# A two-block transformer kernel on one core: the even layer's low rank projection from unsplit fp32 operands, other ring places for later weights, the first gate group's products in another order

## The chip, the core and the metric

The kernel runs on one NeuronCore of a Trainium2 chip. The metric is the device time of one execution, in microseconds (us). Beside it stands one profiled execution, whose trace gives every instruction's start and duration on TensorE (PE, with its weight loads apart as PEld), VectorE (DVE), ScalarE (ACT), GpSimd (POOL) and the DMA queue of SyncE (SP).

## What is computed

The input has 256 tokens of width 1024. The reference runs two blocks. The first is a mixing layer (attention and spatial gating) followed by a feed-forward layer of 16 experts, of which each takes 32 tokens. The second has an even layer and an odd layer. The even layer is the one that the change touches:

```python
def mla_swa_layer(x, positions, g_in, w_in, g_q_a, w_q_up, g_kv_a, w_kv_up, sinks, w_out):
    h = rms_norm(x, g_in)
    z = h @ w_in
    cq, ckv, kpe, q_s, k_s, v_s, gate = split_cols(z, EVEN_SPLITS)   # 256, 128, 32, 512, 128, 128, 1024
    q = (rms_norm(cq, g_q_a) @ w_q_up) ...      # 8 heads of 96
    kv = (rms_norm(ckv, g_kv_a) @ w_kv_up) ...  # 8 heads of 64 + 64
    o_mla = causal_block_attention(qm, km, v_m)
    o_swa = sliding_window_sink_attention(q_s, k_s, v_s, sinks, alibi_slopes(SWA_HEADS))
    o = concatenate([o_mla, o_swa])
    return x + (o * silu(gate)) @ w_out
```

`cq`, `ckv` and `kpe` together are the 416 columns of the low rank projection, called `("e","a")` in the kernel; the queries of the sliding window are `("e","qs")`, its keys and values `("e","kvs")`, and the gate's two halves `("e","g1")` and `("e","g0")`. The two upward projections are `("qup",)` and `("kvup",)`, the output projection `("out2",0)` and `("out2",1)`. The odd layer has units named `("o",...)` and the same gate code.

## The kernel before, in words

**Weights and places.** All weights stream from HBM through a ring of seven places (`ring`, 16 KB of each partition a place), in one fixed order, `unit_of`, which SP issues (L765): each load waits until the unit that owned its place before is used. The experts' weights are plain fp32. The second block's weights are multiplied in another way: each is split into a high part (ACT rounds it, `hi_piece`, L454) and a low part (the rest, `lo_piece`, L466, on DVE or POOL), and a product is the sum of three matmuls, high by high, low by high and high by low (`products`). The high part goes to a second place `hslot`; the low part replaces the weights. A unit therefore takes two places until it is used, and before the change the pairs are `PAIRS`, in turn (3,2), (5,6), (0,1). The activations are split alike: `HE` is (high by ACT at L2016, low by DVE at L1582). The norm's scale is not in `HE`; it is applied to results later (`ra`, `RB`).

**The beginning of the even layer.** When the last expert's product is copied out (L514), PE scatters it to the tokens (L1022), DVE adds it to the transposed residual `XT` in eight pieces of 256 tokens (L1547), and then, piece by piece in the order `KORD`, ACT makes the high activation and a square (L2017), ACT and DVE split the weights of `("e","a")`, DVE makes the low activation. PE multiplies the first 128 tokens piece by piece as they come (L1072, group `("za",0)`), with the matmuls that sum the squares (L1080, two columns each, group `ss`) set between. The second 128 tokens follow (`project`, L496). Then PE runs, in program order: `qst` (`straight`, L508, two groups of 48 matmuls with the rows of the norm, L1090, between), three pairs of transposes, `kst` (L1105), `vst` (L1111), `qup` and `kvup` (L496), and one group of the gate (`gate_matmuls`, L690, four quarters of 12 matmuls). After that it transposes queries and keys (L485) and runs the attention `A2`, with the other gate quarters set between its steps.

**Order on the other engines.** ACT: high parts of `qs`, squares of `za` (L2025), the norm rows (L2029), high parts of `kvs`, `qup`, `kvup`, high part of `CT` (L2037), the copy of `vst` (L516), the copies of the query parts (L2045) with the four pieces of `g1` between, `kvup`'s copies, the pieces of `g0`. POOL: two short steps for the norm, then the low parts of `qup`, `kvup`, `g1`, `g0` and `out2` 0, in steps of 256 columns (16 for each of the last three). A quarter of the gate waits for the low parts of its four input pieces.

## Time and profile before

| | |
|---|---|
| runs | 1386.92 us median of 3 (1386.84 to 1388.49) |
| profiled execution | 1388.61 us, span of the trace 1386.8 us |
| PE, PEld busy | 72%, 37% of the span |
| DVE, ACT, POOL busy | 29%, 17%, 6% |
| HBM read | 480.43 MB, 347 GB/s over the span |
| chain that ended last | DMA 55%, PE 33%, DVE 6%, ACT 3% |

From about 160 us to 1089 us the experts' weights arrive at some 428 GB/s and the transfers set the pace. From 1089 us on the kernel is paced by its engines: the even layer lasts to about 1227 us, the odd layer to the end. Every time below is in us from the start of the span. A PE busy for all of a stretch is not a PE at its peak; the granted clock beside it, 1.00 or 0.50, is the 2.4 or the 1.2 GHz level.

### The profile page before, as it was taken

What the parts mean: (1) busy time and instruction counts of PE and PEld (TensorE: products, weight loads), DVE (VectorE), ACT (ScalarE), POOL (GpSimd) and SP (SyncE); (2) the same over time, 40 slices, a digit from 0 to 9 for tenths busy, and PEclk for the clock granted to TensorE, in tenths of its full rate; (3) what the DMA queues carried; (4) which work ended last, traced back from release to release, by engine and by line L of the source; (5) the groups of instructions that cost most, each with busy time, mean ns of one, the idle gap of its engine ahead of it and who ended that gap; (6) DMA issues with size and microseconds to landing.
All of it is one profiled execution on the core that took longest, in us unless ns stands there. A gap on an engine that the chain in (4) does not pass through costs nothing.

```text
span 1386.8 us, 15261 instructions
## 1 busy us (share of the span) xinstructions
PE 992.9 (72%) x6623; PEld 510.2 (37%) x6623; DVE 396.3 (29%) x954; ACT 239.4 (17%) x483; POOL 89.6 (6%) x129
## 2 busy tenths in 40 slices
PE   4998987666666665566566565666656798899987
PEld 3765842212121111111111111111111487899875
DVE  4756421011111100101011010101101455775584
ACT  3534210000000000000000000000000355643452
POOL 1300000000020000000000000000000044300030
PEclk9999989878887887977888877788877798999998
DMA  9996789999999999999999999999999552144411
GB/s 398 375 378 237 317 362 428 428 429 426 429 427 427 430 427 427 429 427 428 429 428 427 428 428 426 430 428 427 428 427 428 216 184 98 62 182 146 159 62 46
DMA packets 34771, 482.47 MB, mean 348 GB/s; under 512 B 3854, under 2 KB 3856, under 8 KB 5520
## 3 DMA queue, kind: packets, MB, share of 16 engines
q1 hardware_dynamic: 34240, 479.92, 82.7%
q8 instruction: 52, 0.85, 0.2%
q10 hardware_dynamic: 288, 1.05, 0.2%
q0 software_dynamic: 176, 0.53, 0.1%
q14 instruction: 15, 0.12, 0.0%
HBM read 480.43 MB, written 1.05 MB: 347 GB/s over the span
## 4 chain that ended last, share of the span: by engine, by line
DMA 55%; PE 33%; DVE 6%; ACT 3%; issue 1%; POOL 1%; SPq 0%; POOLq 0%; DVEq 0%; ACTq 0%
DMA ring<-in_t_w 52%; PE PS L508 8%; PE PS L1009 6%; PE PS L496 6%; PE PS L1055 3%; DMA ring<-in_t_e_a 2%; DMA ring<-in_t_mod 2%; ACT S L624 1%; PE PS L690 1%; PE PS L485 1%; PE PS L997 1%; PE PS L786 1%; POOL RR L466 1%; PE PS L1022 1%; PE PS L808 1%
## 5 line engine op out<-in xcount | busy, mean ns | idle before, releaser
L1009 PE MATMUL PS<-ring,S 128*32 128x512 f32 x2016 | 320.7, 770 | 213.4 <-DMA ring<-in_t_w 210.9
L1055 PE MATMUL PS<-ring,S 128*32 128x512 f32 x1008 | 168.7, 803 | 103.7 <-DMA ring<-in_t_w 94.8
L1009 PEld LDWEIGHTS PS<-ring,S 128*32 128x32 f32 x2016 | 63.0, 126 | 447.7 <-DMA ring<-in_t_w 329.4
L514 DVE COPY S<-PS 128x512 f32<-128x512 f32 (+2 forms) x47 | 32.1, 682 | 307.9 <-PE PS L1055 287.7
L508 PE MATMUL PS<-SR,RR 128*128 128x256 f32 x736 | 117.5, 285 | 1.2 <-DVE ab L1441 0.9
L1055 PEld LDWEIGHTS PS<-ring,S 128*32 128x32 f32 x1008 | 33.3, 130 | 223.0 <-DMA ring<-in_t_w 147.6
L508 PEld LDWEIGHTS PS<-SR,RR 128*128 128x128 f32 x736 | 103.8, 189 | 2.6 <-DVE ab L1441 1.2
L454 ACT ACTIVATE RR<-ring 128x1024 fp32r<-128x1024 f32 (+3 forms) x95 | 89.5, 1005 | 37.8 <-DMA ring<-in_t_e_a 18.1
L1557 DVE TENSOR_SCALAR S<-PS,KC 128x256 f32<-128x256 f32 x16 | 7.7, 483 | 287.0 <-PE PS L1039 287.0
L516 ACT ACTIVATE S<-PS 128x512 f32<-128x512 f32 (+2 forms) x50 | 27.9, 568 | 340.8 <-PE PS L485 335.9
L466 DVE TENSOR_TENSOR RR<-ring,RR 128x1024 fp32r<-128x1024 f32 (+2 forms) x76 | 84.1, 1154 | 8.5 <-ACT RR L454 8.5
L2004 ACT ACTIVATE S<-PS 128x512 f32<-128x512 f32 x16 | 9.6, 597 | 440.8 <-PE PS L1009 440.8
L496 PE MATMUL PS<-RR,SR 128*128 128x512 f32 (+3 forms) x264 | 76.9, 402 | 0.0
L1567 DVE TENSOR_TENSOR S<-PS,S 128x512 f32<-128x512 f32 x16 | 11.1, 691 | 204.2 <-PE PS L1009 204.2
L485 PE MATMUL PS<-KC,S 128*128 128x128 f32 (+1 forms) x308 | 44.5, 289 | 27.8 <-DVE S L1272 14.8
L508 PE MATMUL PS<-RR,RR 128*128 128x256 f32 x224 | 62.9, 281 | 0.0
L466 POOL TENSOR_TENSOR RR<-ring,RR 128x256 fp32r<-128x256 f32 x74 | 52.5, 743 | 126.3 <-ACT RR L454 126.3
L1547 DVE SCALAR_TENSOR_TENSOR X<-PS,ab,X 128x256 f32<-128x256 f32 x128 | 51.9, 476 | 21.8 <-PE PS L1022 21.8
L690 PE MATMUL PS<-SR,RR 128*128 128x256 f32 x256 | 52.4, 304 | 5.2 <-POOL RR L466 4.6
L485 PEld LDWEIGHTS PS<-KC,S 128*128 128x128 f32 (+1 forms) x308 | 35.7, 146 | 54.9 <-DVE S L1567 35.3
L496 PEld LDWEIGHTS PS<-RR,SR 128*128 128x128 f32 x264 | 51.3, 197 | 11.2 <-issue 0.3
L2173 POOL TENSOR_TENSOR st<-st,KC 128x4 f32<-128x4 f32 x1 | 1.9, 1947 | 714.0 <-DVE st L1591 714.0
(309 smaller groups left out, 986.5 us busy)
## 6 DMA issues: line engine op xcount, KB each, us to landing
ring<-in_t_w SPq DMA_DIRECT2D x189, 2048.0 KB, 31.3
ring<-in_t_mod SPq DMA_DIRECT2D x12, 2048.0 KB, 12.7
ring<-in_t_out SPq DMA_DIRECT2D x6, 2048.0 KB, 7.8
S<-in_t_w SPq DMA_DIRECT2D x3, 2048.0 KB, 12.2
ring<-in_t_e_g SPq DMA_DIRECT2D x2, 2048.0 KB, 7.8
ring<-in_t_o_q SPq DMA_DIRECT2D x2, 2048.0 KB, 7.8
ring<-in_t_o_k SPq DMA_DIRECT2D x2, 2048.0 KB, 8.8
ring<-in_t_o_v SPq DMA_DIRECT2D x2, 2048.0 KB, 8.2
```

The costliest lines, as they stand in the source:

```text
L454: act.e.activation(hi[:, c:c + step, :], dst[:, c:c + step, :], ACT.Copy).then_inc(*act.mark(("hi", key, c)))
L466: t = lane.e.tensor_tensor(lo[:, k, w], place[key][:, k, w], hi[:, k, w].bitcast(F32), ALU.subtract)
L485: t = pe.e.transpose(PS[0:parts, b, 128 * i:128 * i + 128], in_, ident)
L496: m = pe.e.matmul(PS[:, b, 0:width], l_, r_, start=(k == ks[0] and n == 0), stop=(k == ks[-1] and n == 2))
L508: m = pe.e.matmul(PS[:, b, 256 * nn:256 * nn + 256], l_, r_, start=(k == ks[0] and m_ == 0), stop=(k == ks[-1] and m_ == 2))
L514: lane.e.tensor_copy(dst, src).then_inc(*lane.mark(out_of(key), *names))
L516: lane.e.activation(dst, src, ACT.Copy).then_inc(*lane.mark(out_of(key), *names))
L624: t = act.e.activation(p[:, c], p[:, c], ACT.Exp, bias=nm[:, i_:i_ + 1], scale=-1.0, accum_out=sm[:, i_:i_ + 1])
L690: m = pe.e.matmul(PS[:, b, 256 * nn:256 * nn + 256], l_, r_, start=(k == 0 and m_ == 0), stop=(k == 7 and m_ == 2))
L1009: m = pe.e.matmul(PS[32 * j:32 * j + 32, b, :], expert_rows(2 * k + kk, e_, e_ + 1), place[name, e_, k][:, kk, 512 * j:512 * j + 512], sta ...
L1055: m = pe.e.matmul(PS[q:q + 32, b, :], HT[e_ % 2][:, 128 * s + 32 * j:128 * s + 32 * j + 32], place["w2", e_, j][:, s, 512 * dh:512 * dh + ...
L1547: t = dve.e.scalar_tensor_tensor(out=XT[:, k, :], in0=PS[:, banks.of[key], o:o + 256], scalar=ab[:, 7, k:k + 1], in1=XT[:, k, :], op0=ALU. ...
```

## The change

Three edits.

1. **Low rank projection.** The unit `("e","a")` is not split. ACT multiplies its eight pieces (128 by 416, fp32) in place by the gain `gfe`, which used to be in the activations, as soon as the unit has landed. PE multiplies plain fp32 `XT` by these weights: one matmul a piece and token half in the place of three. The order on PE becomes `za` 0, all the square sums, `za` 1. ACT makes the weights, then the four squares, then the eight high activations; DVE adds all eight pieces first and makes the low activations afterwards. The first user of `HE` is then `qst`, which waits for it.
2. **Places.** The later units go to other places: `("e","a")` to 3 alone, `qs` (5,6), `kvs` 0 with both parts, `qup` and `kvup` (1,2), and then (3,5), (6,0), (1,2) in turn. `qup`'s load now follows the last expert unit's use, `g1`'s the use of `("e","a")`, `g0`'s that of `qs`.
3. **Gate.** In the first group of the gate, the quarters are 0 and 1: high by high and high by low activation, for all eight pieces, one output half each; 2 and 3: the low weights by the high activation. The first two wait for the high parts alone. The high pieces of `g1` are now made all together on ACT before the copy of `vst`. The odd layer's first gate group has the same new order.

```diff
-    for n, (key, w) in enumerate(later):
+
+    LATER = [(3, None), (5, 6), (0, 0), (1, 2)] + [((3, 5), (6, 0), (1, 2))[n % 3] for n in range(len(later) - 4)]
+    for (key, w), (slot, hslot) in zip(later, LATER):
         k_ = 2 if key == ("qup",) else 8
-        unit(key, unit_rows("t_" + "_".join(map(str, key)), k_, w), k_, w, *PAIRS[n % 3])
+        unit(key, unit_rows("t_" + "_".join(map(str, key)), k_, w), k_, w, slot, hslot, hoff=2048 if slot == hslot else 0)
...
+                lead = half == halves[0] and n2 == 0
                 for q in range(4):
...
-                    nn = q // 2
+                    nn = q % 2 if lead else q // 2
                     n = 2 * n2 + nn
-                    for k in range(4 * (q % 2), 4 * (q % 2) + 4):
-                        pe.wait_ge(("split", ukey, k))
...
+                    for k in range(8) if lead else range(4 * (q % 2), 4 * (q % 2) + 4):
+                        pe.wait_ge(("hi", ukey, k - k % 2) if lead and q < 2 else ("split", ukey, k))
+                        hi_hi, lo_hi, hi_lo = products(ukey, h, k, slice(128 * n, 128 * n + 128), slice(0, 256), swap=True)
+
+                        group = [hi_hi, lo_hi, hi_lo] if not lead else [hi_hi, hi_lo] if q < 2 else [lo_hi]
...
+        def low_rank(i):
+
+            b = banks.take(("za", i), ALL6)
+            pe.wait_ge(banks.was["za", i])
+            for k in KORD:
+                pe.wait_ge(("weighted", k), ("xa", E - 1, k))
+                m = pe.e.matmul(PS[:, b, 0:416], XT[:, k, 128 * i:128 * i + 128], place["e", "a"][:, k, :], start=k == KORD[0],
+                                stop=k == KORD[-1])
+            m.then_inc(*pe.mark(("za", i), *([used(("e", "a"))] if i else [])))
+
+        low_rank(0)
+        for i in range(2):
+            banks.take(("ss", i), ALL6)
...
         m.then_inc(*pe.mark("ss"))
-        project(pe, ("za", 1), ("e", "a"), HE, 1, 416, ks=KORD, final=True)
+        low_rank(1)
...
-            straight(pe, ("qst", n2), ("e", "qs"), HE, n2, final=n2 == 1)
+            straight(pe, ("qst", n2), ("e", "qs"), HE, n2, final=n2 == 1, first="he")
...
-            lo_piece(dve, ("e", "a"), (0, 4, 2, 6)[c])
-            for k in (c, 4 + c):
-                dve.wait_ge(("he hi", k), "gg", ("xa", E - 1, k))
...
+        for k in KORD:
+            dve.wait_ge(("he hi", k), "gg", ("xa", E - 1, k))
...
         act.stage("even")
-        hi_piece(act, ("e", "a"), 0)
-        hi_piece(act, ("e", "a"), 4)
+        act.wait_ge(("load", ("e", "a")), "gg")
+        for k in KORD:
+            w = place["e", "a"][:, k, :]
+            act.e.activation(w, w, ACT.Copy, scale=gfe[:, k:k + 1]).then_inc(*act.mark(("weighted", k)))
         for c in range(4):
-            for k in (c, 4 + c):
-                act.wait_ge(("xa", E - 1, k), "gg")
-                act.e.activation(HE[0][:, k, :], XT[:, k, :], ACT.Copy, scale=gfe[:, k:k + 1]).then_inc(*act.mark(("he hi", k)))
+            act.wait_ge(("xa", E - 1, c), ("xa", E - 1, 4 + c))
...
+        for k in KORD:
+            act.e.activation(HE[0][:, k, :], XT[:, k, :], ACT.Copy, scale=gfe[:, k:k + 1]).then_inc(*act.mark(("he hi", k)))
         hi_all(act, ("e", "qs"))
...
+        hi_all(act, ("e", "g1"))
         act.wait_ge("vst", ("rcs", 0), ("rcs", 1))
         copy_out(act, "vst", VST, PS[:, banks.of["vst"], 0:256], "vst rows")
...
-            hi_piece(act, ("e", "g1"), 4 * i)
-            hi_piece(act, ("e", "g1"), 4 * i + 2)
```

## Rows read from the trace of the kernel before

**Rows 1.** The page's strips, 40 equal slices: PE clock in tenths, DMA.
```profile
PEclk9999989878887887977888877788877798999998
DMA  9996789999999999999999999999999552144411
```

**Rows 2.** The chain of waits in time order: start, duration, engine and line.
```profile
1059.71 29.61 DMA ring<-in_t_e_a
...
1114.55 5.74 PE PS L508 x48
...
1135.74 0.95 ACT RR L454
1136.76 11.56 POOL RR L466 x16
1148.36 6.37 PE PS L690 x30
...
1303.20 5.77 PE PS L690 x48
```

**Rows 3.** Busy time of PE, PEld, DVE, ACT, POOL; granted clock; DMA; by stretch.
```profile
1092.50:1099.50 7.00, 4.71 (x27) 4.21 (x27) 7.00 (x15) 5.57 (x11) 0.00 (x0) 1.00 0.19 76
1099.50:1106.90 7.40, 7.35 (x29) 7.22 (x30) 2.01 (x3) 3.92 (x5) 0.00 (x0) 0.50 0.00 0
1106.90:1113.10 6.20, 6.20 (x19) 5.92 (x20) 4.72 (x11) 1.02 (x4) 3.24 (x3) 0.50 0.00 0
...
1114.20:1140.30 26.10, 26.10 (x198) 25.21 (x197) 16.01 (x51) 13.04 (x26) 11.84 (x17) 1.00 0.57 212
1140.30:1143.80 3.50, 1.82 (x13) 1.43 (x11) 1.92 (x3) 3.50 (x12) 3.50 (x6) 1.00 0.72 215
...
1148.40:1154.10 5.70, 5.70 (x27) 5.70 (x28) 0.00 (x0) 0.00 (x0) 5.70 (x9) 0.50 0.00 0
```

**Rows 4.** Timeline, PE and its weight loads in the low rank projection.
```profile
1089.41 2.00 PE L1022 MATMUL PS<-S 64*128 64x256 f32 x16 [0.79 <-DVE S L514]
...
1095.58 0.60 PEld L1080 LDWEIGHTS PS<-st,S 128*128 128x128 f32 x4
...
1100.41 1.11 PEld L1080 LDWEIGHTS PS<-st,S 128*128 128x128 f32 x4
...
1113.26 0.54 PE L496 MATMUL PS<-RR,SR 128*128 128x416 f32 x2
...
1113.82 0.54 PE L496 MATMUL PS<-RR,SR 128*128 128x416 f32 x2
```

**Rows 5.** Timeline, PE: four plain fp32 matmuls of 256 columns and what follows.
```profile
1176.98 2.00 PE L1148 MATMUL PS<-S 96*128 96x256 f32 x8
1178.62 0.59 PE L690 MATMUL PS<-SR,RR 128*128 128x256 f32 x2
```

**Rows 6.** Timeline, ACT and DVE as the even layer begins.
```profile
1089.34 1.68 ACT L454 ACTIVATE RR<-ring 128x832 fp32r<-128x832 f32 x2 [18.06 <-DMA ring<-in_t_e_a]
...
1090.16 0.88 DVE L1547 SCALAR_TENSOR_TENSOR X<-PS,ab,X 128x256 f32<-128x256 f32 x2 [0.81 <-PE PS L1022]
...
1090.93 0.89 ACT L2016 ACTIVATE SR<-X,st 128x256 fp32r<-128x256 f32 x2
```

**Rows 7.** Timeline, ACT and POOL before the gate.
```profile
1127.15 1.21 ACT L2037 ACTIVATE SR<-PS,KC 128x256 fp32r<-128x256 f32 x3 [0.78 <-PE PS L485]
1133.31 0.39 ACT L516 ACTIVATE S<-PS 128x256 f32<-128x256 f32 x1 [4.95 <-PE PS L1111]
...
1124.76 7.02 POOL L466 TENSOR_TENSOR RR<-ring,RR 128x256 fp32r<-128x256 f32 x10 [7.62 <-ACT RR L454]
```

**Rows 8.** The page's DMA issues, the gate's two units: KB, us to landing.
```profile
ring<-in_t_e_g SPq DMA_DIRECT2D x2, 2048.0 KB, 7.8
```

**Rows 9.** Timeline, DVE: one step with POOL at rest, then with POOL busy.
```profile
1176.81 0.62 DVE L639 TENSOR_SCALAR S<-S,st 128x256 f32<-128x256 f32 x2
...
1182.10 1.58 DVE L639 TENSOR_SCALAR S<-S,st 128x256 f32<-128x256 f32 x2
```

More of the change, by code:

```diff
@@ L280, in body @@
     FIRST = (3, 4, 2, 7, 8, 5, 6, 0, 1, 9)
-    PAIRS = ((3, 2), (5, 6), (0, 1))
     n_u, borrowed = 0, {}
@@ L295, in body @@
     later += [(("o", n), 512) for n in ("q0", "q1", "k0", "k1", "v0", "v1", "g0", "g1")] + [(("out3", h), 512) for h in range(2)]
-    for n, (key, w) in enumerate(later):
+    LATER = [(3, None), (5, 6), (0, 0), (1, 2)] + [((3, 5), (6, 0), (1, 2))[n % 3] for n in range(len(later) - 4)]
+    for (key, w), (slot, hslot) in zip(later, LATER):
         k_ = 2 if key == ("qup",) else 8
-        unit(key, unit_rows("t_" + "_".join(map(str, key)), k_, w), k_, w, *PAIRS[n % 3])
+        unit(key, unit_rows("t_" + "_".join(map(str, key)), k_, w), k_, w, slot, hslot, hoff=2048 if slot == hslot else 0)
         if key == ("qup",):
-            unit(("kvup",), unit_rows("t_kvup", 1, 1024), 1, 1024, *PAIRS[n % 3], off=1536, hoff=1536, share=key)
+            unit(("kvup",), unit_rows("t_kvup", 1, 1024), 1, 1024, slot, hslot, off=1536, hoff=1536, share=key)
     def used(key):
@@ L683, in gate_matmuls @@
                         pe.wait_ge(banks.was[key])
-                    nn = q // 2
+                    nn = q % 2 if lead else q // 2
                     n = 2 * n2 + nn
-                    for k in range(4 * (q % 2), 4 * (q % 2) + 4):
-                        pe.wait_ge(("split", ukey, k))
-                        for m_, (l_, r_) in enumerate(products(ukey, h, k, slice(128 * n, 128 * n + 128), slice(0, 256),
-                                                               swap=True)):
-                            m = pe.e.matmul(PS[:, b, 256 * nn:256 * nn + 256], l_, r_, start=(k == 0 and m_ == 0),
-                                            stop=(k == 7 and m_ == 2))
+                    for k in range(8) if lead else range(4 * (q % 2), 4 * (q % 2) + 4):
+                        pe.wait_ge(("hi", ukey, k - k % 2) if lead and q < 2 else ("split", ukey, k))
+                        hi_hi, lo_hi, hi_lo = products(ukey, h, k, slice(128 * n, 128 * n + 128), slice(0, 256), swap=True)
+                        group = [hi_hi, lo_hi, hi_lo] if not lead else [hi_hi, hi_lo] if q < 2 else [lo_hi]
+                        for m_, (l_, r_) in enumerate(group):
+                            m = pe.e.matmul(PS[:, b, 256 * nn:256 * nn + 256], l_, r_,
+                                            start=k == 0 and m_ == 0 and (q == 0 or not lead),
+                                            stop=k == 7 and m_ == len(group) - 1 and (q == 3 or not lead))
                     if q == 3:
@@ L1063, in pe_program @@
         pe.stage("even")
-        for name in (("za", 0), ("ss", 0), ("ss", 1)):
-            banks.take(name, ALL6)
-        pe.wait_ge(banks.was["za", 0])
-        for n in range(len(KORD) + 2):
-            if n < len(KORD):
-                k = KORD[n]
-                pe.wait_ge(("split", ("e", "a"), k), ("he", k))
-                for m_, (l_, r_) in enumerate(products(("e", "a"), HE, k, slice(0, 416), slice(0, 128))):
-                    m = pe.e.matmul(PS[:, banks.of["za", 0], 0:416], l_, r_, start=(n == 0 and m_ == 0),
-                                    stop=(n == len(KORD) - 1 and m_ == 2))
-                if n == len(KORD) - 1:
-                    m.then_inc(*pe.mark(("za", 0)))
-            if n >= 2:
-                c, dh = KORD[n - 2] % 4, KORD[n - 2] // 4
-                pe.wait_ge(("sqs", c), "gg", *[banks.was["ss", i] for i in range(2)])
-                for i in range(2):
-                    m = pe.e.matmul(PS[:, banks.of["ss", i], 0:2], sqs[:, c, 256 * dh + 128 * i:256 * dh + 128 * i + 128],
-                                    gg[:, KORD[n - 2], :], start=n == 2, stop=n == len(KORD) + 1)
+        def low_rank(i):
[9 more added lines that the diff above has]
+            banks.take(("ss", i), ALL6)
+        for i in range(2):
+            pe.wait_ge(banks.was["ss", i])
+        for k in KORD:
+            c, dh = k % 4, k // 4
+            pe.wait_ge(("sqs", c), "gg")
+            for i in range(2):
+                m = pe.e.matmul(PS[:, banks.of["ss", i], 0:2], sqs[:, c, 256 * dh + 128 * i:256 * dh + 128 * i + 128],
+                                gg[:, k, :], start=k == KORD[0], stop=k == KORD[-1])
         m.then_inc(*pe.mark("ss"))
-        project(pe, ("za", 1), ("e", "a"), HE, 1, 416, ks=KORD, final=True)
+        low_rank(1)
         def spread_rows(name, n):
```

9 lines of the change are left out of this document (4 added, 5 removed).

## The prediction

> **What bounds the kernel now.** I read the strips first. The transfers are full until the 31st of 40 slices and thin after it, and the clock digit dips until there too [rows 1]: up to about 1089 us the weights set the pace, and nothing of the change touches that, since the units up to the last expert keep their places and their order. The chain of waits then says where the engines take over: the transfer of `("e","a")` ends at 1059.71 + 29.61 = 1089.32, and from there the chain is PE work with two breaks. One is the low rank projection, which ends where `qst` begins, at 1114.4 us on the timeline (the chain, which counts to the end of the last matmul, has 1114.55). The other is POOL: sixteen low pieces of `g1`, 11.56 us, and PE after them at 1148.36 [rows 2]. Third, the table by stretch. In 1092.5 to 1099.5 PE is busy 4.71 of 7.00 us while DVE is busy 7.00 of 7.00: DVE makes two kinds of low part and adds besides. From 1099.5 to 1113.1 PE is full but at clock 0.50. From 1114.2 to 1140.3 it is full at clock 1.00, 26.10 of 26.10. Then the gate: half idle (1.82 of 3.50), and at clock 0.50 up to 1154.1 [rows 3]. So between 1089.4 and 1154.7 there are two places to gain in, and 26 us between them that only move.
>
> **Part 1, the low rank projection.** It removes the eight splits of `("e","a")` on ACT and DVE, 48 matmuls of the split form and every wait of PE for a low part here. It adds eight ACT steps of 128 by 416 and 16 plain fp32 matmuls of 416 columns.
>
> ACT: 128 by 832 takes 1.68 / 2 = 0.84 us, 128 by 256 takes 0.89 / 2 = 0.45 us [rows 6]; 416 lies between, about 0.55. They start with the landing at 1089.3, so the first is there at 1089.9 and the last at 1093.7. DVE's eight additions at 0.44 [rows 6] run from 1090.2 to 1093.7. PE is in the scatter from 1089.4 and free at about 1091.3 [rows 4]. So PE never waits for either: it takes a piece in more time than they do.
>
> PE: a plain fp32 matmul shows as two records. Eight records of 256 columns take 1178.62 - 1176.98 = 1.64 us, 0.205 each [rows 5]; for 416 columns that is 0.33. The split form shows 1113.82 - 1113.26 = 0.56 us for three matmuls of 416 columns at full clock [rows 4], 0.19 each. If the 128 by 128 fp32 weight load is not hidden behind the matmul before, 0.60 / 4 = 0.15 us comes on top [rows 4]: 0.48 a record. I take 0.36, near the lower end, since at [rows 5] the weight loads are of the same kind and are hidden. Then one token half is 16 x 0.36 = 5.8 us against 24 x 0.19 = 4.5: PE has 2.6 us more work, and the reason for a gain is the waits alone. The squares' matmuls are paced by their weight loads, 32 x 0.15 = 4.8 us at full clock and 32 x 0.28 = 9 us at half [rows 4]; their operands are there (four squares on ACT after 1093.7, about 0.6 each, to 1096.1).
>
> At full clock: 1091.3 + 5.8 + 4.8 + 5.8 = 1107.7 for the first matmul of `qst`, 6.7 us sooner than 1114.4. `qst` needs the high and low activations and split weights: ACT 1096.1 + 8 x 0.45 = 1099.7, DVE just behind, then the `qs` pieces on ACT to 1103.6 and on DVE to about 1106.5, each piece before PE wants it. The norm's chain starts from the end of the squares, 1101.9 where it was 1107.1, so the rows are ready too.
>
> **The clock** takes part of this back. It fell at 1099.5 after a stretch in which PE worked 4.71 of 7.00 us, two-column matmuls among them. It then stayed at 0.50 through 7.40 us in which PE was 7.35 us busy, mostly alternating with the squares' matmuls, and came back only after 6.2 us of dense 416-column work; the gate's stretch shows the same, 5.7 us dense before the rise [rows 3]. That PE was busy was thus not enough there, and the squares' matmuls were much of what it did. The change puts 4.8 us of them in one block. I expect the clock to fall in that block or at its end, and to come back after some 6 us of `za` 1. Those 6 us do 3 us of work: 3.0 lost. If the fall comes in the middle of the block, its second half costs 1.8 more. I take the mean, 3.9 lost: `qst` at 1111.6, **2.8 us sooner**. The bounds are 6.7 sooner (no fall) and 10.8 later (below).
>
> Here the Trainium skill speaks otherwise ("TensorE: Matmul & The Clock Gate", section "Why this matters for your kernels"): keep TensorE continuously busy, without long idle gaps, and the clock stays up. The new order has no idle gap, so by it there is no fall. The trace agrees in part: it shows a full clock in the 26 us without gaps, but also half clock through a stretch with PE busy. I follow the trace, and give the rule's result as a rival.
>
> **Part 2, places.** No work is added, only loads come sooner. `g1` waits for the use of `("e","a")` (1111.6 or before) and lands 7.8 us later [rows 8], at 1119.4, where it is wanted at about 1125. Its high parts need the place of `qs`, used at the end of `qst`, before that as well. `g0` follows `qs` and lands by about 1132; wanted at 1138. From `out2` on each unit waits for the same unit as before, so the rest of the rotation costs and brings nothing. Early loads share the queue with nothing that is awaited: price 0; if `g1` were late, ACT would stand at its high parts with the copy of `vst` and all query copies queued behind it, and 4 us of slack would have to go first.
>
> **Part 3, the gate.** Times in this part are those of before; all of it moves by 2.8. ACT stands idle from the high part of `CT`, done at 1128.4, to `vst` at 1133.3 [rows 7]. The four high pieces of `g1` at 0.97 fit, 1128.4 to 1132.3. POOL ends its first ten steps at 1124.76 + 7.02 = 1131.8 [rows 7] and goes on with `g1` at once, 5 us sooner than 1136.76: 11.56 us [rows 2], done at 1143.3. PE reaches the gate at 1140.3 [rows 3] and has 32 matmuls that want high parts only, 32 x 0.12 = 3.8 us, to 1144.1. By then all low parts are there, and the other 16 end at 1146.1. As a whole that is 5.77 us, as the same 48 matmuls without a wait take in the odd layer [rows 2]. Before, the group ended at 1148.36 + 6.37 = 1154.73 [rows 2], or 1154.6 by starts, so it took 14.3 us. **8.5 us sooner**, of which about 2.8 us is that the clock no longer falls here. What is late next: the query copies on DVE end at 1140.7 and the key parts at 1142.2, both ahead of 1146.1; ACT, rid of the interleaved pieces, ends its copies at 1141. The attention follows as it stood, and its low parts of `g0` are ready sooner relative to it. In the odd layer the group already runs without a wait [rows 2], so the new order gives 0 there.
>
> **POOL beside DVE.** POOL now works from 1131.8 to 1136.8, where it rested and DVE scales the residual in eight steps of two SBUF operands. The trace shows what such company can cost: a pair of DVE steps takes 0.62 us with POOL at rest and 1.58 with it busy [rows 9], 0.5 each. Eight steps would lose about 4 us, of which the slack to 1146.1 hides nearly all. I take 0.5 us, with 0 and 2 as ends. The Trainium skill ("SBUF — State Buffer", section "SBUF: two separate sides") says that a DVE step with two SBUF inputs and a GpSimd step that reads SBUF lock each other out entirely. By that POOL too would lose eight DVE steps of 0.4 us, 3.2 us, and quarter 3 would wait; the sum would be some 1.5 us smaller. No row shows POOL much slowed: 0.70 a step beside DVE, 0.72 here.
>
> **Sum.** 2.8 + 8.5 - 0.5 = 10.8 us. The profiled execution, 1388.6 us, would become 1377.8. The median of the runs was 1386.92, 1.7 us under it, and a new median should be **1376.1**.
>
> **Rivals.**
> - *The clock holds.* No fall in the block of squares: 3.9 us more gain, 1372.2. For it: PE is dense for 5.8 us before the block. Against: the fall at 1099.5 and the low stretch with PE full [rows 3].
> - *The gate gains less.* POOL starts `g1` no sooner, because the high parts come late or DVE holds it up: then the low parts end at 1148.4, PE follows with the last matmuls to 1149.5, and the gain is 5.1 in the place of 8.5: 1379.5. So would it be if the change failed to do what it says.
> - *Plain fp32 is dearer.* Weight loads in the open, 0.48 a record: 32 x 0.12 = 3.9 us more, 1380.0.
> - *Slower.* The clock is low from the scatter to the end of the projection. Then 1.9 + 11.6 us of work double to 27 and the squares take 9: 1089.4 + 36 = 1125.2, 10.8 later than 1114.4, less 8.0 from the gate: 2.8 us slower, 1389.7. It decides from about 14.5 us of loss to the clock, and needs nearly the whole stretch at 0.50. Before, only 13.6 us of it were.
>
> **How the numbers follow.** Forecast 0.53, clock holds 0.22, gate gains less 0.11, dearer fp32 0.10, slower 0.04. The range takes in the first two with the ends of the clock's loss and the third and fourth: 1371.8 to 1380.2, which leaves out something under 2 in 10. About 0.2% of the time, 2.8 us, is what a measurement can tell from no change. All cases but the last are faster by more than that; with something for cases that I do not see: faster 0.93, same 0.03, slower 0.04.
>
> **What would show it.** `qst`'s first matmul near 1111.6 (1107.7 if the clock holds), and two-column matmuls in one block with the clock falling in or right behind it. PE without a wait from 1091.3 on. POOL's low parts in one run of 26 steps with no idle before `g1`. The gate's first group about 5.8 us long at full clock, and the transposes behind it near 1143.8. Wrong would be: fp32 records of 416 columns over 0.4 us apart, ACT waiting before `vst`, PE waiting in quarter 2, or a new loss in the attention that eats what was won.

## The result, and the profile after

The changed kernel took 1378.55 us, the median of six runs (1376.87 to 1384.31), beside 1386.88 us for the kernel before, run beside it (six runs, 1386.84 to 1388.56): a ratio of 0.9942, interval 0.9925 to 0.9959. Run again beside the experiments it had 1379.43 and 0.9934 [0.9917, 0.9951]. So it is about 8.3 us faster by the medians and 8.0 by the ratio (5.7 to 10.4), where 10.8 were forecast. The time lies in the range, 2.4 us above the number. That small distance is in part luck: it hides errors that cancel in part.

The page of the kernel after: the span, the busy engines, the strips and the shares of the chain.

```profile
span 1382.5 us, 15237 instructions
...
PE 993.8 (72%) x6607; PEld 505.7 (37%) x6607; DVE 397.5 (29%) x950; ACT 240.9 (17%) x487; POOL 91.1 (7%) x129
...
PEclk9999989788787788778687887888887899999999
DMA  9896789999999999999999999999999733154411
...
DMA 55%; PE 35%; DVE 6%; ACT 3%; issue 1%; SPq 0%; POOL 0%; POOLq 0%; DVEq 0%; ACTq 0%
```

The page alone says little: as in [rows 1] the transfers are full up to the 31st slice. This profiled execution, 1384.31 us, was the slowest of the six; those of the experiments lie up to 8 us apart from it. The comparison is therefore made by stage. Each stage below is read off the timeline by first starts, so that the sum of a line is the span: the end of DVE's copy of the last expert's product; from there to the first matmul of `qst`; from `qst` to the first matmul of the gate; the gate's first group; the rest. The last column is the span less the first, which is free of how soon the weights came in that execution (1088.0 to 1091.8 us, by the execution and not by the edit).

| profile | copy ends | to `qst` | to gate | gate group | rest | from copy to end |
|---|---|---|---|---|---|---|
| before | 1089.4 | 25.0 | 25.9 | 14.3 | 232.2 | 297.4 |
| after | 1091.8 | 19.9 | 31.5 | 5.6 | 233.6 | 290.7 |
| e5_changed_again | 1089.4 | 19.9 | 31.6 | 5.7 | 233.3 | 290.5 |
| e2_pool_later | 1088.2 | 19.8 | 26.3 | 12.8 | 235.0 | 293.9 |
| e4_places_gate_only | 1089.5 | 27.4 | 29.7 | 5.7 | 233.5 | 296.5 |
| e3_low_rank_only | 1088.0 | 19.9 | 26.2 | 13.5 | 231.8 | 291.4 |
| e1_scaling_later | 1088.8 | 16.5 | 26.2 | 5.7 | 238.5 | 286.9 |
| e7_scaling_split | 1088.8 | 20.0 | 26.2 | 6.1 | 235.9 | 288.2 |
| e11_scaling_split_again | 1090.0 | 19.8 | 26.2 | 6.1 | 234.2 | 286.3 |
| e8_old_gate_order | 1089.2 | 16.5 | 31.4 | 5.7 | 233.5 | 287.2 |
| e9_split_old_order | 1088.5 | 16.5 | 26.3 | 9.6 | 233.8 | 286.2 |
| e6_squares_last | 1088.4 | 16.8 | 34.5 | 5.7 | 233.5 | 290.5 |
| e10_squares_between | 1091.5 | 16.5 | 27.9 | 5.9 | 232.8 | 283.0 |

Two stages gained, 5.1 and 8.7 us, and the one between them, where nothing was to happen, lost 5.6: 8.2 in all. The rest took 1.4 us more, so that from the copy on the profile is 6.7 us shorter; in e5_changed_again it is 6.9. The medians differ by 8.3. The chain of waits of the kernel after shows them (start, duration, engine and line; L1075 is the low rank projection, L1088 the squares' matmuls, L509 `qst`, L497 `kvup`, L694 the gate):

```profile
1091.10 0.70 DVE S L515
1091.85 2.00 PE PS L1027 x16
1093.85 5.78 PE PS L1075 x16
1099.63 4.41 PE PS L1088 x32
1104.04 8.10 PE PS L1075 x16
1112.14 5.71 PE PS L509 x48
...
1129.76 6.75 DVE X L1642 x8
1136.51 0.63 DVE st L525
1137.24 0.63 DVE st L527
...
1139.48 3.90 PE PS L497 x9
1143.38 5.63 PE PS L694 x48
1149.01 3.53 PE PS L486 x32
...
1299.44 5.71 PE PS L694 x48
```

From the copy on PE goes from the scatter into the projection, the squares and the projection again without a gap, where [rows 3] had PE busy 4.71 of 7.00 us. The gate's 48 matmuls follow one another in 5.63 us; the POOL step of [rows 2] that they used to wait for is gone from the chain. The odd layer's group takes 5.71, against 5.77 in [rows 2]. New in the chain are 6.75 us of DVE at L1642, which scales the residual.

The windows of the kernel after, columns as in [rows 3], give the clock:

```profile
1093.80:1099.50 5.70, 5.70 (x20) 3.15 (x18) 2.85 (x9) 5.70 (x13) 0.00 (x0) 1.00 0.69 285
1099.50:1103.90 4.40, 4.40 (x33) 4.40 (x32) 3.69 (x8) 4.40 (x8) 0.00 (x0) 0.78 0.08 33
1103.90:1108.80 4.90, 4.90 (x8) 2.50 (x9) 4.57 (x11) 1.96 (x5) 3.24 (x3) 0.50 0.00 0
1108.80:1111.70 2.90, 2.90 (x11) 1.59 (x9) 0.15 (x1) 0.39 (x2) 0.00 (x0) 1.00 0.00 0
...
1135.80:1139.50 3.70, 0.17 (x2) 0.02 (x1) 3.67 (x13) 0.76 (x3) 3.70 (x6) 1.00 0.01 2
1143.20:1148.80 5.60, 5.60 (x49) 5.58 (x48) 0.00 (x0) 4.44 (x6) 3.71 (x6) 1.00 0.81 284
```

The clock is full in `za` 0, falls in the block of squares (a mean of 0.78), stays at 0.50 into `za` 1 and is back by 1108.8. The fifth line is the new wait: PE works 0.17 of 3.70 us while DVE and POOL are both full.

### The profile page after: what moved, and what is told of

It reads as the page before. It is cut to its first block, busy times and chain, and to the rows that moved or that the text cites. A ratio compares the mean times of both kernels' runs of the same rounds, so it can differ in the third digit from the quotient of the medians.

```text
span 1382.5 us, 15237 instructions
## 1 busy us (share of the span) xinstructions
PE 993.8 (72%) x6607; PEld 505.7 (37%) x6607; DVE 397.5 (29%) x950; ACT 240.9 (17%) x487; POOL 91.1 (7%) x129
## 4 chain that ended last, share of the span: by engine, by line
DMA 55%; PE 35%; DVE 6%; ACT 3%; issue 1%; SPq 0%; POOL 0%; POOLq 0%; DVEq 0%; ACTq 0%
DMA ring<-in_t_w 54%; PE PS L509 8%; PE PS L1014 6%; PE PS L497 5%; PE PS L1060 3%; DMA ring<-in_t_mod 2%; PE PS L486 1%; PE PS L694 1%; ACT S L625 1%; PE PS L1075 1%; PE PS L1027 1%; PE PS L791 1%; PE PS L1002 1%; PE PS L813 1%; PE PS L589 1%
## 5 line engine op out<-in xcount | busy, mean ns | idle before, releaser
L509 PE MATMUL PS<-SR,RR 128*128 128x256 f32 x736 | 118.0, 286 | 1.0 <-DVE ab L1449 0.9
L509 PEld LDWEIGHTS PS<-SR,RR 128*128 128x128 f32 x736 | 104.3, 190 | 2.5 <-DVE ab L1449 1.2
L455 ACT ACTIVATE RR<-ring 128x1024 fp32r<-128x1024 f32 (+2 forms) x91 | 85.9, 1006 | 20.0 <-DMA ring<-in_t_o_v 17.0
L467 DVE TENSOR_TENSOR RR<-ring,RR 128x1024 fp32r<-128x1024 f32 (+1 forms) x72 | 80.1, 1162 | 8.6 <-ACT RR L455 8.6
L497 PE MATMUL PS<-RR,SR 128*128 128x512 f32 (+2 forms) x248 | 70.7, 397 | 3.5 <-DVE S L1659 3.5
L509 PE MATMUL PS<-RR,RR 128*128 128x256 f32 x224 | 63.2, 282 | 0.0
L497 PEld LDWEIGHTS PS<-RR,SR 128*128 128x128 f32 x248 | 46.7, 191 | 14.8 <-DVE S L1659 4.0
L694 PE MATMUL PS<-SR,RR 128*128 128x256 f32 x256 | 49.8, 293 | 0.6 <-DVE SG L743 0.6
```

Of the source, the lines that this page charges most:

```text
L455: act.e.activation(hi[:, c:c + step, :], dst[:, c:c + step, :], ACT.Copy).then_inc(*act.mark(("hi", key, c)))
L467: t = lane.e.tensor_tensor(lo[:, k, w], place[key][:, k, w], hi[:, k, w].bitcast(F32), ALU.subtract)
L497: m = pe.e.matmul(PS[:, b, 0:width], l_, r_, start=(k == ks[0] and n == 0), stop=(k == ks[-1] and n == 2))
L509: m = pe.e.matmul(PS[:, b, 256 * nn:256 * nn + 256], l_, r_, start=(k == ks[0] and m_ == 0), stop=(k == ks[-1] and m_ == 2))
L694: m = pe.e.matmul(PS[:, b, 256 * nn:256 * nn + 256], l_, r_, start=k == 0 and m_ == 0 and (q == 0 or not lead), stop=k == 7 and m_ == len( ...
```

## The experiments

### Where the middle stretch lost

PE's timeline names the releaser (start, duration, line, operation, output and operands, count, and in brackets the wait before it), DVE's and POOL's show what they did. First the kernel after:

```profile
1139.48 1.22 PE L497 MATMUL PS<-RR,SR 128*128 128x512 f32 x2 [3.53 <-DVE S L1659]
...
1129.76 6.75 DVE L1642 SCALAR_TENSOR_TENSOR X<-X,KC,cvec 128x256 f32<-128x256 f32 x8
1136.43 0.71 DVE L525 TENSOR_TENSOR st<-S,rcs 128x32 f32<-128x32 f32 x1
...
1122.33 19.91 POOL L467 TENSOR_TENSOR RR<-ring,RR 128x256 fp32r<-128x256 f32 x26 [7.59 <-ACT RR L455]
```

then the same two kinds of DVE step in the kernel before, where POOL was at rest:

```profile
1132.19 3.26 DVE L1635 SCALAR_TENSOR_TENSOR X<-X,KC,cvec 128x256 f32<-128x256 f32 x8
1135.37 0.18 DVE L524 TENSOR_TENSOR st<-S,rcs 128x32 f32<-128x32 f32 x1
```

Beside POOL the eight scaling steps take 6.75 us in place of 3.26, and a rotary step of 32 columns 0.71 in place of 0.18 (three of the six such steps do; the three between them keep 0.18). Steps of the same stretch that read one operand from PSUM are not slowed: those of 80 columns take 0.23 to 0.24 us beside POOL and without it. Behind them DVE copies and rotates the queries, which frees the PSUM banks of `qup`; `kvup` takes one of these banks, and PE waits 3.53 us for it. The theory: POOL, which now makes the low parts of `g1` 5 us sooner, holds up DVE, and that holds up PE by a bank. The rival: the wait comes from the new places or the late start of the projection.

**e1_scaling_later** moves the eight scaling steps out of the way.

```diff
-        dve.wait_ge(*[("sqs", c) for c in range(4)], *[("he", k) for k in range(8)])
-        for k in range(8):
-            t = dve.e.scalar_tensor_tensor(out=XT[:, k, :], in0=XT[:, k, :], scalar=c_gf[:, k:k + 1], ...)
-        t.then_inc(*dve.mark("x2"))
...
         dve.wait_ge(out_of(("kvup", 1, 1)))
         t.then_inc(*dve.mark("km"))
+        dve.wait_ge(*[("sqs", c) for c in range(4)], *[("he", k) for k in range(8)])
+        for k in range(8):
+            t = dve.e.scalar_tensor_tensor(out=XT[:, k, :], in0=XT[:, k, :], scalar=c_gf[:, k:k + 1], ...)
+        t.then_inc(*dve.mark("x2"))
```

> The changed kernel with DVE's eight scaling steps of the residual (x2) moved behind the key parts. Theory A (in the changed kernel the scaling, slowed by POOL beside it, keeps DVE from freeing the banks of the query projection, and PE waits 3.5 us for a bank in the key and value projection): the wait is gone, from the first matmul of qst to the first of the gate it is 26 us again in the place of 31.6, and the time falls by about 5 us against the changed kernel, to some 1373 us. Rival B (PE's wait there is for something else, or the scaling only costs later what it cost before): still over 30 us from qst to gate or the loss found again before the attention, time within 1 us of the changed kernel's 1378.

**e2_pool_later** leaves DVE as it is and holds POOL instead, until DVE has made the key parts.

```diff
+        pool.wait_ge("km")
         lo_all(pool, ("e", "g1"))
```

> The changed kernel with POOL's low parts of g1 held back until DVE has made the key parts (km). Theory A (POOL is what slows DVE's scaling): the eight scaling steps take 3.3 us again in the place of 6.75, PE has no wait before the gate, but the gate's quarters 2 and 3 now wait for POOL, which ends some 11.5 us after the key parts; gate's end about 2 to 3 us later than in the changed kernel, time about 1380. Rival B (the scaling is slow for another reason, such as its place against ACT or PE): it stays at 6.75 us, and the time goes up by 6 us or more, to 1384 and over.

Measured: e1 1377.55 us, ratio 0.9932 [0.9909, 0.9955]; e2 1381.98, 0.9963 [0.9950, 0.9975]. DVE in e2, then in e1:

```profile
1126.18 3.26 DVE L1642 SCALAR_TENSOR_TENSOR X<-X,KC,cvec 128x256 f32<-128x256 f32 x8
1129.36 0.18 DVE L525 TENSOR_TENSOR st<-S,rcs 128x32 f32<-128x32 f32 x1
```

```profile
1132.59 7.12 DVE L1665 SCALAR_TENSOR_TENSOR X<-X,KC,cvec 128x256 f32<-128x256 f32 x8
1139.63 0.68 DVE L730 TENSOR_TENSOR SG<-PS,cvec 128x512 f32<-128x512 f32 x1
```

With POOL silent the steps are at their old 3.26 and 0.18 us, PE does not wait for a bank, and the stretch takes 26.3 us, with the places and the projection of the change. So POOL's company is the cause, and 5.2 us of the 5.6 hang on it. e1 takes the steps out of `kvup`'s path and has 26.2 too. But neither gives the whole gain. In e2 POOL is now late for the gate, which takes 12.8 us in place of 5.6, 6.8 us of it and of what follows at half clock:

```profile
1133.68 12.45 POOL L467 TENSOR_TENSOR RR<-ring,RR 128x256 fp32r<-128x256 f32 x18 [7.94 <-DVE S L1665]
...
1144.80 2.50 PE L694 MATMUL PS<-SR,RR 128*128 128x256 f32 x10 [2.23 <-POOL RR L467]
```

In e1 the steps are still beside POOL, 7.12 us, and now stand before DVE's first step on the gate (L730): from the end of the gate's group to the first exponential of the attention it takes 10.0 us in place of 7.4 (6.6 in e5). The 5 us over the change that were expected of e1 did not come: the median is 1.0 to 1.9 us under the changed kernel's two.

The 7.4 us are themselves 1.0 longer than in the kernel before (6.4), and that is POOL's company once more. A DVE step of four columns ahead of the first exponential, first after, then before:

```profile
1155.05 1.17 DVE L607 SCALAR_TENSOR_TENSOR st<-KC,st 128x4 f32<-128x4 f32 x1
```

```profile
1160.78 0.16 DVE L606 SCALAR_TENSOR_TENSOR st<-KC,st 128x4 f32<-128x4 f32 x1
```

In the kernel after POOL is still at the low parts of `g0`, until 1156.20, and the step ends at 1156.22; in the kernel before POOL had ended at 1159.32.

### The parts alone

**e4_places_gate_only** is the kernel before with edits 2 and 3 and the old projection; **e3_low_rank_only** is the kernel after with the old places and the old gate, `g1`'s high pieces between the query copies again. e4 against the kernel before, then e3 against the kernel after:

```diff
+    LATER = [(3, 2), (5, 6), (0, 0), (1, 2)] + [((3, 5), (6, 0), (1, 2))[n % 3] for n in range(len(later) - 4)]
+                    nn = q % 2 if lead else q // 2
...
+        hi_all(act, ("e", "g1"))
         act.wait_ge("vst", ("rcs", 0), ("rcs", 1))
```

```diff
-    LATER = [(3, None), (5, 6), (0, 0), (1, 2)] + [((3, 5), (6, 0), (1, 2))[n % 3] for n in range(len(later) - 4)]
+    LATER = [(3, None)] + [((3, 2), (5, 6), (0, 1))[n % 3] for n in range(1, len(later))]
...
-        hi_all(act, ("e", "g1"))
...
+            hi_piece(act, ("e", "g1"), 4 * i)
+            hi_piece(act, ("e", "g1"), 4 * i + 2)
```

> The kernel before with edits 2 and 3 alone (places, high parts of g1 together and earlier, new order in the first gate group; the low rank projection split as before, its high parts in place 2). Theory A (the gate's 8.5 us are won, but DVE beside POOL gives back 5 to 6 us before the gate): 3 us faster than before, 1384 us, with the scaling steps at over 6 us and a wait of PE of about 3.5 us before the gate. The prediction's own term (8.5 less 0.5): 8 us faster, 1379 us, with no wait before the gate.

> The kernel before with edit 1 alone (plain fp32 projection; the places of the other units, the high parts of g1 and the order in the gate as before). By the changed kernel's trace, in which qst began 19.9 us after the landing of the unit against 25.1 before: 5 us faster than before, 1382 us, and the gate's group at 14 us as before. By the prediction's own term: 2.8 us faster, 1384 us. A rival that the clock gives all of it back: 1386.9.

Measured: e4 1388.19 us, ratio 0.9995 [0.9981, 1.0009]; e3 1382.35, 0.9965 [0.9952, 0.9977]. The places and the gate alone bring nothing that can be measured, where 3 us were expected. In e4's profile the gate's group is 8.6 us shorter, the stretch before it 3.8 longer, and the projection 2.4 longer, with the clock low for 20.5 us from 1095.0 where it was low for 13.7 before. The longer projection, with that longer low stretch, is what the expectation did not have. The same wait as in the kernel after is there, with the old projection, so the new projection is not its cause; the new places are not either, since e2 has them and no wait:

```profile
1134.78 6.75 DVE L1640 SCALAR_TENSOR_TENSOR X<-X,KC,cvec 128x256 f32<-128x256 f32 x8
...
1144.51 0.73 PE L497 MATMUL PS<-RR,SR 128*128 128x512 f32 x2 [3.54 <-DVE S L1657]
```

The projection alone, e3, is worth 4.9 us by the ratio and 5.1 in its stage. Its chain, the scatter first and then the same 16, 32 and 16 records as above:

```profile
1088.01 3.70 PE PS L1024 x16
1091.71 5.78 PE PS L1072 x16
1097.49 3.47 PE PS L1085 x32
1100.96 7.39 PE PS L1072 x16
1108.35 5.71 PE PS L509 x48
```

The scatter takes 3.70 us in place of 2.00, because the clock was at 0.50 until 1091.5; behind the block it was low for 3.4 us more, against 6.8 in the kernel after.

From the copy to the end the profiles of the parts, 6.0 us shorter (e3) and 1.0 (e4), add up to about the change's 6.7. By the ratios, 4.9 and 0.7 against 8, they fall some 2.5 us short; e4's twelve runs lie between 1380.64 and 1391.54, so that this is not told from their spread.

### The same kernel again

**e5_changed_again** is the changed kernel without an edit, to see what of a profile repeats.

> The changed kernel once more, beside the next three on one chip. 8 us faster than the kernel before. From the first matmul of qst to the first of the gate 31 to 32 us, the gate's first group 5.7 us. Theory on its spread (1376.9 to 1384.3 us in six runs): the time from the landing of the last expert weights to qst differs from run to run with the place of the low clock, 17 us without one and 20 us with one; a rival is that the spread comes from the experts' stage alone.

Measured: 1379.43 us. Its stages repeat those of the first profile within 0.3 us, 19.9, 31.6 and 5.7; the copy ended 2.4 us sooner. So these stages are the kernel's own as far as two profiles can tell, and the landing of the weights is the execution's. The expectation set the spread of the runs down to a fall of the clock that comes in some executions only; both profiles have the fall, so that they do not decide it, and the copy alone moved by 2.4 us.

### Both engines apart: half of the scaling on each side

**e7_scaling_split**, and once more **e11_scaling_split_again**, put four scaling steps where POOL still rests, ahead of DVE's low parts of `kvs`, and four behind the key parts.

```diff
+        dve.wait_ge(("rb", "e"), *[("sqs", c) for c in range(4)], *[("he", k) for k in range(8)])
+        for k in range(4):
+            dve.e.scalar_tensor_tensor(out=XT[:, k, :], ...)
         lo_all(dve, ("e", "kvs"))
...
         t.then_inc(*dve.mark("km"))
+        for k in range(4, 8):
+            t = dve.e.scalar_tensor_tensor(out=XT[:, k, :], ...)
+        t.then_inc(*dve.mark("x2"))
```

> The changed kernel with the eight scaling steps split: four right before the low parts of kvs, where POOL rests, four behind the key parts. In the first experiment all eight behind the key parts took 7.1 us beside POOL and held the gate's first DVE step up by about 2 us. Theory A: the first four take 1.6 us, the last four 3.4 us or less and end before the gate's group does; PE has no wait before the gate (26 us from qst to gate), and transposes follow the group at once. 6 to 8 us faster than the changed kernel, about 1371 us. Rival: the low parts of kvs come later now, and PE waits for them in kst, up to 1 us, or the first four still meet POOL: then no better than the first experiment, within 1 us of its time.

> e7 once more, beside the two above. Theory (what e7 wins before the gate is kept, and its profile lost 3 us to two low stretches of the clock in the odd layer's attention by where they fell): 26.2 us from qst to gate, 6.1 for the group and 226 to 229 us from the first exponent to the end, median about 1376 to 1378, 10 to 12 us faster than before. Rival (the loss in the odd layer belongs to the schedule): 229 us again there.

Measured: 1378.81 us, 0.9922 [0.9908, 0.9937], and 1377.20, 0.9922 [0.9899, 0.9944]. DVE in e11:

```profile
1117.68 1.67 DVE L1620 SCALAR_TENSOR_TENSOR X<-X,KC,cvec 128x256 f32<-128x256 f32 x4 [2.76 <-ACT cvec L2039]
...
1137.51 3.60 DVE L1668 SCALAR_TENSOR_TENSOR X<-X,KC,cvec 128x256 f32<-128x256 f32 x4
```

One kernel holds both prices: 0.42 us a step with POOL at rest, 0.90 beside it. The stretch before the gate takes 26.2 us in both profiles, and the path from the gate to the first exponential 6.5, so nothing of e1's loss is left. From the copy to the end the profiles are 2.5 and 4.4 us shorter than that of the kernel after. Up to the first exponential both are 5.7 to 5.8 us ahead of the kernel after. The rest of it goes in low stretches of the clock in the odd layer, 10.2 us of them in e7 where the kernel after has 3.4; in e11, which has 3.4 there too, 1.0 us goes between the first exponential and the odd layer's gate and 0.5 behind it. By the ratios the gain over the change is 1.7 to 2.8 us, where 6 to 8 were expected of e7, and it is within the intervals.

### What the order of the gate's products is worth

**e8_old_gate_order** is the kernel after with the old order of the first group; **e9_split_old_order** is e7 with the old order.

```diff
-                    nn = q % 2 if lead else q // 2
+                    nn = q // 2
...
-                    for k in range(8) if lead else range(4 * (q % 2), 4 * (q % 2) + 4):
-                        pe.wait_ge(("hi", ukey, k - k % 2) if lead and q < 2 else ("split", ukey, k))
+                    for k in range(4 * (q % 2), 4 * (q % 2) + 4):
+                        pe.wait_ge(("split", ukey, k))
```

> The changed kernel with the old order of products in the gate's first group (each quarter waits for its low parts). Theory (as PE is held up before the gate anyway, POOL has ended g1's low parts at 1142.2 before the gate starts at 1143.2, so the order brings nothing): the group takes 5.7 us as in the changed kernel, time within 1 us of it. The prediction's own view, in which the group reaches high parts 3 us before the low parts are there: 1 to 3 us slower than the changed kernel.

> The kernel with the scaling split (four steps before the low parts of kvs, four behind the key parts) and the old order of products in the gate's first group. In e7, with the new order, PE came to the gate without a wait and the group took 6.1 us. Theory (now the order counts, since the high parts are there and POOL is not yet through with g1's low parts): the group takes 8 to 9 us here, 2 to 3 us more than in e7, and the transposes follow that much later. Rival (POOL is through before PE comes to the gate in this schedule too): 5.7 to 6.1 us, as in e7.

Measured: e8 1380.69 us, 0.9942 [0.9926, 0.9957], the ratio of the changed kernel itself; e9 1376.99, 0.9921 [0.9907, 0.9936], that of e7. In e8 the group takes 5.7 us with the old order. It begins at 1137.1, and POOL has the last low part of `g1` at 1136.3 (two of the 26 records are missing from the trace):

```profile
1117.84 18.46 POOL L467 TENSOR_TENSOR RR<-ring,RR 128x256 fp32r<-128x256 f32 x24
```

So in the change the sooner high and low parts did all of the gate's gain, and the new order had nothing to hide, because PE came late by the very wait that POOL caused. With PE on time the order does work in the profile: the group takes 9.6 us in e9, behind a wait for a low part, and 6.1 in e7 and e11.

```profile
1135.96 0.79 PE L692 MATMUL PS<-SR,RR 128*128 128x256 f32 x2 [2.34 <-POOL RR L467]
```

Part of these 3.5 us is a fall of the clock behind that wait (records of the same kind start 0.21 us apart at first and 0.12 later). The medians do not separate the two, so that the order is worth anything in the whole time stays unshown.

### The squares and the clock

Nine profiles have the block of squares between `za` 0 and `za` 1. In six of them (after, e2, e3, e5, e7, e11) the clock fell in the block or up to 1.1 us behind it, and `qst` came 19.8 to 20.0 us after the copy; in three (e1, e8, e9), with the same instructions on PE there, it held, and `qst` came after 16.5. Four of the six (after, e2, e5, e11) lose all of it to one low stretch of 6.8 us. In e3 and e7 the low stretch behind the block is 3.4 us, and the other half of the loss lies in the scatter, which ran at half clock. The block and `za` 1 in e1, columns as in [rows 3]:

```profile
1096.60:1100.10 3.50, 3.50 (x34) 3.50 (x33) 3.04 (x6) 3.50 (x7) 0.00 (x0) 1.00 0.07 28
1100.10:1105.30 5.20, 5.20 (x17) 2.81 (x17) 4.81 (x12) 2.78 (x6) 3.25 (x3) 1.00 0.00 0
```

 One theory: the block of two-column matmuls brings the fall. The rival: the fall has nothing to do with them. **e6_squares_last** moves the block behind `za` 1; **e10_squares_between** is e7 with the four matmul records of each piece's squares ahead of its `za` 1 piece. The two edits in turn:

```diff
         low_rank(0)
+        low_rank(1)
         for i in range(2):
             banks.take(("ss", i), ALL6)
...
         m.then_inc(*pe.mark("ss"))
-        low_rank(1)
```

```diff
+        for k in KORD:
+            pe.wait_ge(("sqs", k % 4), "gg")
+            for i in range(2):
+                m = pe.e.matmul(PS[:, banks.of["ss", i], 0:2], sqs[...], gg[:, k, :], ...)
+            m = low_rank_piece(1, k)
```

> The changed kernel with the block of the squares' matmuls behind the second half of the low rank projection. Theory C (the block of two-column matmuls makes the clock fall): where the clock falls, it falls in or behind the block, now in the first 6 us of qst, and costs the same 2 to 3 us there; time within 2 us of the changed kernel. Rival D (the fall has to do with the idle time before the scatter, and the block with nothing): the fall stays at the same distance from the scatter, now inside the projection's dense part. Both expect the norm's chain, 5.6 us later, to hold up nobody: it has the first group of qst as cover.

> e7 with the squares' matmuls set between the eight pieces of the second token half of the projection, four records before each piece, in the place of a block ahead of them. Theory C (it is the unbroken block of two-column matmuls that lets the clock fall; it fell in or behind it in six of eight profiles with the block ahead of a dense part): no fall before qst or a shorter one, from the copy of the last expert product to qst 16.5 to 17.5 us, where it was 19.9 to 20.0 with a fall. Rival D (their amount counts, wherever they stand, as in the kernel before, where they were set between and the clock fell too): a fall as before, 19.5 us or more to qst, perhaps longer than in the block's case.

Measured: e6 1381.33 us, 0.9943 [0.9931, 0.9956]; e10 1375.55, 0.9916 [0.9898, 0.9934]. The windows of e6 and then of e10, columns as before:

```profile
1090.50:1101.80 11.30, 11.30 (x34) 6.21 (x35) 6.44 (x14) 11.19 (x20) 0.00 (x0) 1.00 0.36 149
1101.80:1105.20 3.40, 3.40 (x34) 3.40 (x32) 0.00 (x0) 0.00 (x0) 0.00 (x0) 0.99 0.72 217
1105.20:1112.00 6.80, 6.58 (x30) 6.29 (x31) 4.72 (x11) 2.04 (x8) 3.51 (x5) 0.50 0.47 200
```

```profile
1091.50:1098.00 6.50, 6.49 (x29) 4.04 (x30) 3.30 (x9) 6.50 (x14) 0.00 (x0) 1.00 0.80 313
1098.00:1107.90 9.90, 9.90 (x51) 7.00 (x50) 4.64 (x11) 6.47 (x11) 0.00 (x0) 1.00 0.08 31
```

In e6 the projection runs at full clock through 11.3 us; then the block comes, PE busy 3.40 of 3.40 us, and the clock is at 0.50 right behind it, now in `qst`. The fall moved with the block: to `qst` 16.8 us in place of 19.9, to the gate 34.5 in place of 31.5. That the block brings the fall is thus shown once by moving it. In e10 there is no fall. But e1, e8 and e9 had none with the block whole, and before, with the same matmuls in between, it fell [rows 3]; so one profile does not show that the mixing prevents it. It has a price, too: the first group of `qst` now waits for DVE's low parts of `qs` and takes 7.3 us in place of 6.1, so that 1.6 us go before the gate (27.9 against 26.2).

Nor is it shown what decides between a fall and none for the same instructions. One thing divides the nine profiles, and no run varied it: in the six with a fall the block began 5.8 to 8.0 us after the clock had last come back to full, in the three without one 8.1 to 8.6 us. It is not a plain matter of more or less, since in e6 the block began 13.6 us after and the clock fell.

e10 has the best median of all, 1375.55 us, 3 to 4 us under the changed kernel's two (by the ratios, each to the kernel before on its own chip, 2.5 to 3.6), and its profile is the shortest from the copy to the end, 283.0 us. Its interval overlaps those of the others.

## Why the prediction was right or wrong

**What bounds.** Right in the main. The edits moved time between 1089 and 1155 us, as read from [rows 1 to 3]. But the rest of the kernel took 1.4 and 1.1 us more in the two profiles of the change, and 0.4 less in e3, and the prediction had it follow as it stood. Of the 1.4, 1.0 is the DVE step beside POOL ahead of the first exponential (0.2 of the 1.1 in e5_changed_again). From there to the odd layer's gate it takes 1.0 more in both profiles, and from that gate to the end 0.6 and 0.1 less. I did not settle what these are; the low stretches of the clock lie elsewhere in every profile there.

**Part 1, the projection: right mechanism, mis-sized.** PE without a wait, ACT's and DVE's steps off its path, and 5.8 us for a token half are there (5.78). The record of 0.36 us, taken from [rows 5] rather than with an open weight load, was right: they start 0.35 apart. Three terms were too dear. The squares take 3.47 us at full clock (e3), 0.11 a record, not 0.15: the 0.60 us of [rows 4] run to the end of the last of four loads, and three of these start 0.11 apart. That is 1.3 us. `za` 1 takes 5.35 us by starts (e1), not 5.8: 0.5. And the clock took 3.4 us (19.9 against 16.5 without a fall), not 3.9: 0.5 again. With these 2.3 the 2.8 us sooner become 5.1, and without a fall the 6.7 become 8.5. The clock fell where the prediction said, in or at the end of the block. By the Trainium skill ("TensorE: Matmul & The Clock Gate", section "Why this matters for your kernels") a TensorE kept busy would have kept its clock; the windows of after and e6 show a fall out of a stretch in which it was busy all of the time, e1, e8, e9 and e10 show none. The rival "the clock holds" is what three of the nine executions with the block did, and its price of 3.9 was 3.4.

**Part 2, places.** Priced at 0. No run changed the places alone; the only wait of PE before the gate in the profile after is the one for the bank. But the 0 hides what the places did. `g1` landed at 1134.70 in the kernel before, so that with the old places POOL could not have gone on to it at 1131.8; after, it landed at 1120.40. The gate's gain rests on that, and so does the loss.

**Part 3, the gate: right in its time, wrong in its reason.** The group took 5.6 to 5.7 us (forecast 5.77) and gained 8.7 (forecast 8.5), with the clock full. POOL went through 26 steps in one run, as said. The prediction had PE reach the gate before the low parts were ready, and the new order cover the difference. PE arrived after them, and e8 shows the same group without the new order.

**POOL beside DVE: the term that failed.** The prediction had the eight steps, the rate from [rows 9] (0.5 us lost each; 3.49 / 8 = 0.44 measured), and "about 4 us, of which the slack to 1146.1 hides nearly all". The rate was good and the slack was wrong. It was counted to the end of the gate, where the query copies are wanted by the transposes. But the copies also free the banks of `qup`, and `kvup` takes them ahead of the gate. That consumer was not on the list, and it has no slack: 3.53 us of wait and, behind it, some 1.7 us at half clock (26.2 against 31.5 in all). It also left out the rotary steps, three of which took 0.71 us in place of 0.18, and the step ahead of the first exponential. The term was 0.5, the loss before the gate 5.2 to 5.6.

The Trainium skill ("SBUF — State Buffer", section "SBUF: two separate sides") says that the two lock each other out for whole instructions. For DVE the trace agrees, 3.26 to 6.75 us. For POOL it agrees in part. Seven steps beside the scaling in the kernel after, then eight ahead of it:

```profile
1130.04 6.19 POOL L467 TENSOR_TENSOR RR<-ring,RR 128x256 fp32r<-128x256 f32 x7
```

```profile
1123.06 5.61 POOL L467 TENSOR_TENSOR RR<-ring,RR 128x256 fp32r<-128x256 f32 x8
```

That is 0.88 us a step against 0.70. One DVE and one POOL step then go together each 0.88 us, which is less than the 0.40 and 0.69 that they take alone, one behind the other. So POOL lost some 0.2 us a step where the rule gave it 0.4. The prediction's 0.72 was a mean over sixteen steps, and hid that two of them, beside DVE's two steps of 256 columns at 1139.2 to 1140.8, started 0.89 and 0.87 apart. The sum by that rule, 1.5 us smaller, was the nearer one, though by quarter 3 waiting, which did not happen.

**The sum.** Forecast 2.8 + 8.5 − 0.5 = 10.8; measured 5.1 + 8.7 − 5.6 = 8.2 in the stages that it names. The projection gave 2.3 more than its term and POOL's company took 5.1 more than its own; that these cancel by half, and keep the time in the range, is luck. No rival describes it: "the gate gains less" gave 1379.5, near the 1378.55 measured, but by a gate that came late, and it came on time. The slower rival was far off, since no profile had the clock low throughout; e4 came nearest, with 20.5 us and the old projection, and was level with the kernel before.

## What to carry to other kernels

When an engine's work moves in time, list everyone who waits for the engine that it will now run beside, the releases of PSUM banks too, and take the slack to the first of them, not to the stage that the change is about. Where VectorE and GpSimd must both work, give VectorE's steps on SBUF operands a time in which GpSimd rests (those that read PSUM went on undisturbed here): split so, the scaling had neither the lost stretch of the change nor the late start of the attention of e1, though the medians are too close to rank them. And before an order of products is credited with a gain, put back the old order alone: here the sooner operands had done it, and they came from the new places.

## What the runs showed of the hardware

VectorE pays for GpSimd's company by the step, and small steps pay the most for their size: 0.41 to 0.84 us for 256 columns with two SBUF operands, 0.18 to 0.71 for 32 columns (three steps of six), 0.16 to 1.17 for 4. Steps that read one operand from PSUM kept their 0.23 to 0.24 us. GpSimd pays less but not nothing, 0.70 to 0.88 a step while VectorE's steps of 256 columns run beside it.

A plain fp32 matmul of 416 columns costs two records of 0.35 us, 0.70, against 0.56 for three split ones [rows 4], and saves all that makes the parts. Two-column fp32 matmuls in a row, each record with its own weight load of 128 by 128, start 0.11 us apart at full clock.

TensorE's clock fell to its 1.2 GHz level in or right behind 3.4 to 4.6 us in which TensorE was busy throughout with two-column matmuls, and the same instructions kept 2.4 GHz in other executions. A low stretch of 6.8 us costs 3.4 us in this stage, one of 3.4 us half of that. Such differences, and the end of the copy, which moves by up to 3.8 us, are of the size by which the runs of one kernel lie apart (7.4 and 6.9 us for the change), so that no single profile told a gain of 2 us.
